# Two-layer encoder on one Trainium2 core: order of gate products, first gather and sums of squares

## What is computed

```python
def encoder_trunk(x, p, W):
    h = x
    for i in range(DEPTH):                       # layer 0: mla_mixer, layer 1: gdn_mixer
        hn = rmsnorm(h, W['norm_mix_g'][i])
        h = h + (mla_mixer if i % 2 == 0 else gdn_mixer)(hn, ...)
        h = h + expert_choice_moe(rmsnorm(h, W['norm_ffn_g'][i]), ...)
        gate = jax.nn.sigmoid(rmsnorm(h, W['norm_ple_g'][i]) @ W['ple_w_gate'][i])
        h = h + (p[i] @ W['ple_w_proj'][i]) * gate
    return rmsnorm(h, W['final_norm_g'])

def expert_choice_moe(h, w_router, w_gate, w_up, w_down):   # 16 experts, 32 tokens of each sequence
    aff = jax.nn.softmax((xt @ w_router), axis=-1)
    gate, idx = lax.top_k(aff.T, cap)
    xe = jnp.take(xt, idx, axis=0)
    hid = silu(xe @ w_gate) * (xe @ w_up)
    ye = (hid @ w_down) * gate[..., None]        # added back at idx

def gdn_mixer(h, w_in, conv_w, A_log, dt_bias, norm_g, w_out):
    # proj = h @ w_in: q, k, v (3072 columns), z (1024), b, a
    # conv of 5 taps and silu on q, k, v; q and k divided by their l2 norm over each head
    # o = chunk_gated_delta forward + backward, rmsnorm(o) * silu(z), @ w_out
```

## Time and profile before

| | us |
|---|---|
| time, median of 3 runs | 1766.92 (1766.44 to 1767.38) |
| the profiled execution's own time | 1766.45 |
| its span, first to last instruction | 1764.7 |
| PE busy | 1636.6 (93% of the span) |
| DVE / ACT / POOL busy | 572.2 / 453.6 / 133.0 |
| mean granted TensorE clock | 0.982 |
| moved by DMA | 450.34 MB, mean 255 GB/s |

### The profile page before, as it was taken

One profiled execution on the slowest core, in us unless ns is written; L12 is line 12 of the kernel. 1 busy time (PEld: TensorE's weight loads), 2 busy tenths in 40 slices (PEclk: granted clock), 3 DMA queues, 4 the chain that ended last, 5 costly groups with the idle time before them and its releaser, 6 DMA issues.

```text
span 1764.7 us, 21301 instructions
## 1 busy us (share of the span) xinstructions
PE 1636.6 (93%) x9045; PEld 847.3 (48%) x9045; DVE 572.2 (32%) x1030; ACT 453.6 (26%) x990; POOL 133.0 (8%) x113
## 2 busy tenths in 40 slices
PE   7999899999889979999999899898999998899788
PEld 4464544443233324578875677854444432333233
DVE  3562311121201213388971356633111212012032
ACT  3232211101011105422125565442111010111053
POOL 2000000000000002052404231000000000000000
PEclk9999999999999999999999999999999999999999
DMA  7008379999999995012120000264799999999931
GB/s 251 1 1 333 120 316 427 427 427 428 427 425 427 428 424 191 1 48 96 50 94 1 1 3 2 97 282 171 286 428 427 427 429 428 424 427 428 426 132 48
DMA packets 50909, 450.34 MB, mean 255 GB/s; under 512 B 4931, under 2 KB 7199, under 8 KB 25599
## 3 DMA queue, kind: packets, MB, share of 16 engines
q1 hardware_dynamic: 50288, 448.67, 61.3%
q0 software_dynamic: 288, 0.22, 0.0%
q10 hardware_dynamic: 239, 0.09, 0.0%
HBM read 446.87 MB, written 2.10 MB: 254 GB/s over the span
## 4 chain that ended last, share of the span: by engine, by line
PE 68%; DMA 15%; DVE 7%; ACT 5%; issue 4%; POOL 1%; SPq 1%; DVEq 0%; ACTq 0%; POOLq 0%
PE banks L1830 28%; PE banks L1241 13%; DMA ring<-in_moe_w_up 7%; PE banks L1369 5%; DMA ring<-in_moe_w_down 5%; PE banks L1463 3%; PE banks L1721 3%; PE banks L1809 3%; PE banks L1858 2%; DVE misc L2171 2%; DMA ring<-in_moe_w_gate 2%; PE banks L1886 2%; PE banks L1324 1%; PE banks L1428 1%; PE banks L1513 1%
## 5 line engine op out<-in xcount | busy, mean ns | idle before, releaser
L1830 PE MATMUL banks<-ring,misc 128*64 128x512 f32 x2048 | 458.2, 598 | 34.0 <-DMA ring<-in_moe_w_up 21.0
L1830 PEld LDWEIGHTS banks<-ring,misc 128*64 128x64 f32 x2048 | 146.6, 138 | 318.3 <-issue 276.6
L1830 PE MATMUL banks<-ring,hid_t 128*64 128x512 f32 x976 | 217.5, 595 | 16.1 <-DMA ring<-in_moe_w_down 13.4
L1241 PE MATMUL banks<-ring,xt 128*128 128x512 f32 (+1 forms) x448 | 189.8, 585 | 1.0 <-ACT xt L830 0.5
L2537 DVE TENSOR_TENSOR work<-work,banks 128x512 f32<-128x512 f32 x32 | 33.6, 1052 | 476.7 <-PE banks L1830 476.7
L1191 ACT ACTIVATE misc<-banks 32x512 f32<-32x512 f32 x64 | 37.6, 587 | 458.3 <-PE banks L1830 457.9
L1830 PEld LDWEIGHTS banks<-ring,hid_t 128*64 128x64 f32 x976 | 68.4, 137 | 155.5 <-issue 138.1
L1241 PEld LDWEIGHTS banks<-ring,xt 128*128 128x128 f32 x448 | 84.8, 190 | 104.0 <-issue 102.9
L2552 DVE COPY misc<-banks 32x512 f32<-32x512 f32 x64 | 44.2, 691 | 226.0 <-PE banks L1830 225.6
L678 POOL TENSOR_TENSOR ring<-ring 128x1024 f32<-128x1024 f32 x24 | 59.6, 2486 | 738.9 <-DMA ring<-in_gdn_w_in 666.4
L2171 DVE SCALAR_TENSOR_TENSOR misc<-ring,conv_w,misc 128x512 f32<-128x512 f32 x96 | 92.2, 960 | 3.4
(11 more groups left out here) (327 smaller groups left out, 1677.0 us busy)
## 6 DMA issues: line engine op xcount, KB each, us to landing
ring<-in_moe_w_gate SPq DMA_DIRECT2D x64, 2048.0 KB, 22.3
ring<-in_moe_w_up SPq DMA_DIRECT2D x64, 2048.0 KB, 24.0
ring<-in_moe_w_down SPq DMA_DIRECT2D x58, 2048.0 KB, 25.0
ring<-in_gdn_w_in SPq DMA_DIRECT2D x8, 2048.0 KB, 8.4
ring<-in_ple_w_gate SPq DMA_DIRECT2D x4, 2048.0 KB, 21.4
ring<-in_moe_w_down SPq DMA_DIRECT2D x6, 1024.0 KB, 23.2
ring<-in_mla_w_out SPq DMA_DIRECT2D x2, 2048.0 KB, 23.4
misc<-in_moe_w_down SPq DMA_DIRECT2D x2, 2048.0 KB, 21.4
```

Source lines behind the costliest of these rows:

```text
L1241: mm = pe.matmul(psum[:, banks.bank(st, i), 0:cols], lhs(k), rhs(k), start=(k == 0), stop=(k == n - 1))
L1830: mm = pe.matmul(psum[64 * f:64 * f + 64, bank, :], tokens(4 * kh + k), w[k][:, k, f * HALF:(f + 1) * HALF], start=(kh == 0 and k == 0), s ...
```

## The change

In three places the order of work is changed. What is computed stays the same.

1. Experts, both layers: part 3 of the first gather runs behind piece 0's products, in front of piece 1's, and the wait for DVE's reading of it stands in front of the seventh of the eight feature blocks. Pieces 9 and 10 trade slots, and SP issues piece 10 (2 MB, into piece 0's slot) ahead of the half of piece 9 (1 MB, into piece 1's).
2. Projection, blocks 1 to 4: the sums of squares run behind P7.
3. Core: the gates stand in portions of three steps and are through before the last two pairs of `build_qk` products of p = 0. On ACT, `end_levels(p)` runs behind the first `spread_u` of the next pass.

PE at the start of the experts of layer 0, before and now. L1809 (now L1808) is the gather, L1830 (now L1831) the products with a piece; 8 matmuls are one piece.

```diff
--- before.py
+++ after.py
@@ -380,7 +380,7 @@
 
             if m == EXTRA:
                 return NSLOT
-            n = m - (m > EXTRA)
+            n = {EXTRA + 1: 9, EXTRA + 2: 8}.get(m, m - (m > EXTRA))
             return place(l, n if n < NARROW else (4, 5, 6, 7, 0, 1)[(n - NARROW) % 6])
 
         def user_before(m):
@@ -426,7 +426,7 @@
                             banks.add(s_bat, 0)
                         if u == 0 and x == P3:
                             banks.add(s_cum, 0)
-                        if 1 <= u <= 4 and x == P2:
+                        if 1 <= u <= 4 and x == P7:
                             banks.add(s_nrm, u - 1)
                         if u == 5 and x == P2:
                             banks.add(s_nt, 0)
@@ -594,7 +594,7 @@
                 sp.wait_ge(*L.s_lg.full(1))
                 src = expert_w["down"][l, 0].rearrange("(a p k) n -> p a k n", a=2, k=4)
                 sp.dma_start(second_down, src[:, 1, 0:2, :]).then_inc(second_in, 16)
-                for m in range(EXTRA + 1, NPIECE):
+                for m in (EXTRA + 2, EXTRA + 1, *range(EXTRA + 3, NPIECE)):
                     if m == NARROW + 7:
 
                         sp.wait_ge(moe_sem["w_used"], last_user(2) + 1 + L.done["w_used"])
@@ -1057,6 +1057,7 @@
                     if live:
                         spread_u(p, 0)
                     if p:
+                        end_levels(prev)
                         keep(apply_banks, "z5", prev, c_z5, 32)
                         spread_inverse(prev)
                     else:
@@ -1110,8 +1111,6 @@
                     if p == 0:
                         gate_in(6)
                         gate_in(7)
-                    if live:
-                        end_levels(p)
 
                 def turned(k):
 
@@ -1397,14 +1396,6 @@
                                                start=True, stop=True)
                         mm.then_inc(s_cum.filled, 1)
                     block_product(u, P2, a12, b21)
-                    if 1 <= u <= 4:
-                        b = u - 1
-                        pe.wait_ge(sq16, 4 * b + 4)
-                        banks.claim(pe, s_nrm, b)
-                        for g in range(4):
-                            mm = pe.matmul(psum[32 * g:32 * g + 32, banks.bank(s_nrm, b), :], pick[:, b, :], sqb[:, g, :],
-                                           start=True, stop=True)
-                        mm.then_inc(s_nrm.filled, 1)
                     if u == 5:
                         s_nrm.wait_read(pe, 3)
                         banks.claim(pe, s_nt, 0)
@@ -1415,6 +1406,14 @@
                         pe.wait_ge(x_comb_pool, 2)
                     pe.wait_ge(w_comb_done, 4 * u + 4)
                     block_product(u, P7, s3, t3)
+                    if 1 <= u <= 4:
+                        b = u - 1
+                        pe.wait_ge(sq16, 4 * b + 4)
+                        banks.claim(pe, s_nrm, b)
+                        for g in range(4):
+                            mm = pe.matmul(psum[32 * g:32 * g + 32, banks.bank(s_nrm, b), :], pick[:, b, :], sqb[:, g, :],
+                                           start=True, stop=True)
+                        mm.then_inc(s_nrm.filled, 1)
                     block_product(u, P4, a22, t4)
 
                 def gate_part(i, k0, k1):
@@ -1641,13 +1640,14 @@
                         dt5(prev)
                     else:
                         gate_part(5, 5, KD)
+                        gate_part(6, 0, 1)
                     if live:
                         level_turn(p, 1)
                         level_z(p, 2)
                     if p:
                         z6(prev)
                     else:
-                        gate_part(6, 0, 2)
+                        gate_part(6, 1, 4)
                         build_kk(1, 0)
                     if p >= 2:
                         for a in range(4):
@@ -1662,7 +1662,7 @@
                     if 1 <= p < QS:
                         du6(prev)
                     elif p == 0:
-                        gate_part(6, 2, 4)
+                        gate_part(6, 4, 7)
                         build_kk(1, 1)
                     if build:
                         build_kk(p + 1, 0)
@@ -1676,7 +1676,8 @@
                         for a in (0, 1):
                             new_values(prev, a)
                     else:
-                        gate_part(6, 4, 6)
+                        gate_part(6, 7, KD)
+                        gate_part(7, 0, 2)
                         build_kk(1, 2)
                     if build:
                         build_kk(p + 1, 1)
@@ -1690,7 +1691,7 @@
                         for a in range(4) if odd else (2, 3):
                             new_values(prev, a)
                     else:
-                        gate_part(6, 6, KD)
+                        gate_part(7, 2, 5)
                         build_kk(1, 3)
                     if build:
                         build_kk(p + 1, 3)
@@ -1703,13 +1704,11 @@
                         for a in range(4):
                             attend(prev, a)
                     else:
-                        gate_part(7, 0, 4)
+                        gate_part(7, 5, KD)
                     if live:
                         build_qk(p, 0)
                         build_qk(p, 1)
                         level_d(p, 4)
-                        if p == 0:
-                            gate_part(7, 4, KD)
                         build_qk(p, 2)
                         build_qk(p, 3)
                 def project_heads(i, half):
@@ -1789,9 +1788,9 @@
                                                start=(t == 0), stop=(t == NT - 1))
                     mm.then_inc(gcol_in, 1)
 
-                def gather(q):
-
-                    for kp in range(4):
+                def gather(q, kps=range(4)):
+
+                    for kp in kps:
                         if q and kp < 2:
                             if q >= 2:
                                 pe.wait_ge(moe_sem["scat_free"], 8 * (q - 1) + L.done["scat_free"])
@@ -1810,7 +1809,7 @@
                                                    start=(t == 0), stop=(t == NT - 1))
                         mm.then_inc(moe_sem["gather_in_psum"], 1)
 
-                def unit_product(kind, n, bank, tokens):
+                def unit_product(kind, n, bank, tokens, ahead={}):
 
                     for kh in range(2):
                         m = piece(kind, n, kh)
@@ -1824,6 +1823,8 @@
                         else:
                             pe.wait_ge(loaded[r], 16 * (L.base[r] + nth_load(l, m)))
                         for k in range(4):
+                            if 4 * kh + k in ahead:
+                                ahead[4 * kh + k]()
                             if k == 2 and m in (EXTRA + 1, NPIECE - 1):
                                 pe.wait_ge(loaded[r], 16 * (L.base[r] + nth_load(l, m)))
                             for f in range(2):
@@ -1887,17 +1888,29 @@
                                            start=(k == 0), stop=(k == 1))
                         mm.then_inc(moe_sem["pp_in_psum"], 1)
 
-                gather(0)
+                def gathered(parts, *engines):
+
+                    for who in engines:
+                        pe.wait_ge(moe_sem["gather_read_" + who], parts + L.done["gather_read_" + who])
+
+                def rest_of_gather():
+
+                    gather(0, (3,))
+                    gathered(2, "act")
+
+                gather(0, (0, 1, 2))
+                gathered(1, "act", "dve")
                 for ex in range(NE + 1):
                     if ex < NE:
                         q, i = ex // GRP, ex % GRP
-                        if i == 0:
+                        if i == 0 and q:
                             for who in ("act", "dve"):
                                 pe.wait_ge(moe_sem["gather_read_" + who], 2 * (q + 1) + L.done["gather_read_" + who])
                         if ex >= 2:
 
                             pe.wait_ge(moe_sem["hid_done"], ex - 1 + L.done["hid_done"])
-                        unit_product("gate", ex, 2 * (ex % 2), lambda k: xg[:, q % 2, k, i, :])
+                        unit_product("gate", ex, 2 * (ex % 2), lambda k: xg[:, q % 2, k, i, :],
+                                     {} if ex else {4: rest_of_gather, 6: lambda: gathered(2, "dve")})
                     if ex:
                         turn_hidden(ex - 1)
                     if ex < NE:
```

## The result

| | before | after |
|---|---|---|
| median, us | 1767.03 (1766.44 to 1767.38, 4 runs) | 1750.79 (1749.03 to 1752.55, 4 runs) |
| the profiled execution's own time | 1766.45 | 1752.55 |
| its span | 1764.7 | 1750.8 |
| PE / DVE busy | 1636.6 / 572.2 | 1636.9 / 575.0 |
| mean granted clock | 0.982 | 0.982 |

What follows compares the result with a forecast made beforehand. Bound: products with expert pieces (28% of the span) and waits for their transfers (14%), elsewhere PE and its waits. Terms 5.0 + 2.0 + 3.9 + 4.6 = 15.5 us, from median 1766.92 to 1751.4; range 1745.5 to 1758.5.

Steps and rivals of the forecast that it cites:

- Stream, 5.0 forecast: Experts' piece transfers: stream starts 2.3 to 2.8 us earlier, taken as 2.5 us a layer, 5.0 for both.
- A gap again, not a larger one than before, or larger by half a us: Experts, first loads: 2 MB then 1 MB are issued before pieces 1 and 2 are used, leaving this transfer gap.
- my lower bound of 2.3: Experts: low end of the 2.3 to 2.8 us a layer by which the stream starts earlier.
- no extra one at 266 us: Experts: piece 10 is used at about 263.7, loads issued last to about 266.7, so its later wait is hidden.
- Projection, 2.0 forecast: Blocks 1 to 4: of 4.6 + 0.6 us about 2.0 remain, since DVE cannot follow; bounds 5.2 and 0.
- the 4.6 us: Projection, block 1: the 3.12 us wait for squares and the low clock behind it go, 4.6 us together.
- Core, p = 0 to 1, 3.9 forecast: Gates end 2.9 us earlier; d of the second level comes at 1010.2 in place of 1014.12, 3.9 us.
- PE has no wait in that pass: Core, p = 0: total of gate products unchanged and PE never waits there.
- the case that DVE's predicated copy is held: Core, p = 0 to 1: copy held until 997.6 by POOL's clearing, `build_qk` waits, turn 1.9 us later, 2.0 remain.
- Core, p = 1 to 3, 4.6 forecast: Two passes: 1.1 us sure at low clock, 3.5 if the clock stays up; one of each, 4.6 us.
- Even at each place: Core, p = 1 to 2 and 2 to 3: even odds that the clock falls behind waits of 0.5 and 1.3 us.
- The first rival: Core: clock falls in both passes and DVE's copy is held, 4.2 in place of 8.5; time 1755.7; chance 0.27.

Runs made afterwards that it cites:

- the first profile: Profile of the whole change against the kernel before, first comparison; ratio 0.9916, median 1750.79 us, the profiled execution 1752.55 us.
- the second: Profile of the whole change measured once more, unaltered, as base of three later kernels; ratio 0.9916 (0.9902 to 0.9931) to the kernel before.

## Why the prediction was right, and where it wasn't

The total held, 15.5 forecast against 14.8 (12.7 to 17.1), and each part gained; but the terms were off on both sides. That the total came within 0.7 us is partly luck: the errors below have both signs, and the terms of the core were reckoned from one profile of before, in which the clock happened to be kind from p = 0 to 1.

**Stream, 5.0 forecast, 4.0 found.** The start was right (2.8, found 2.86). The step that failed is "A gap again, not a larger one than before, or larger by half a us": from the first issue to the last load it takes about 0.9 us longer than before (409.1 to 409.8 us against 408.4 to 408.7). 2.0 us are kept a layer, below my lower bound of 2.3. In the kernel with the stream alone this loss is there by 300 us, so it belongs to the first loads. No second gap came at piece 10, and no extra one at 266 us. The trade of slots, which I had counted into the same sum, is worth 1.3 us a layer, but only together with the moved gather.

**Projection, 2.0 forecast, 2.65 found** (204.10 to 201.44). The mechanism was right and the size of the waits was off: squares late in blocks 2, 3 and 4, POOL's sums over whole convolutions. The waits were 1.2, 0.4 and 0.9 us for my 1.6, 0.5 and 1.3, 2.5 in place of 3.4, and that is the difference; the new waits didn't lower the clock (the interval is 201.41 to 201.44 in four profiles). What I had not seen is how much of the 4.6 us was chance. Waits alone give 3.12 + 0.28 + 0.27 - 2.52 = 1.15 us, which is 202.58 less 201.43; the rest is the low clock behind the old wait, 0 to 2.8 us.

**Core, p = 0 to 1, 3.9 forecast, 3.65 found** (19.44 to 15.40, less 0.39). The 0.39 us are a step I put at nothing ("PE has no wait in that pass"): the first turn of p = 1 comes later (42.58 to 42.97), because PE waits for a bank of `build_qk` that DVE still reads, now that no gate products stand between d and the last pair. I had named this wait, but only for the case that DVE's predicated copy is held. It wasn't: the copy took 0.80 us beside the 3.51 us of clearing, and 0.78 us before, without it:

```profile
991.54 0.78 DVE L2270 COPY_PREDICATED misc<-blocks,misc 128x256 f32<-128x256 uint8 x2 [3.82 <-ACT misc L978]
```
The rule of the Trainium skill (SBUF — State Buffer, "SBUF: two separate sides") holds here, and the rival's half that hung on it didn't come. The 3.65 us are luck in one respect: three profiles with the old gates show 19.4 to 19.5 us at this place, three others 21.1 to 22.0, by the clock behind the same wait of 4.07 us. Against these the change gives 5.3 to 6.3 us. The gates alone leave 17.65 us, with 1.85 us of waiting for ACT's spread, which stands behind end_levels there; with end_levels moved it is 15.40.

**Core, p = 1 to 3, 4.6 forecast, 3.0 in the first profile, 5.9 in the second.** 21.38 to 19.15 and 20.56 to 19.75; then 21.38 to 19.18 and 20.56 to 16.85. With the clock up a pass gives 3.7 us, forecast 3.5. But that is against a pass of before with the clock low; against the two old ones of 18.51 us with the clock up it gives 0.8, what the shorter waits give by themselves. With the clock low I had put 1.1; it was 2.2 at p = 1 to 2, and 0.8 or 2.2 at p = 2 to 3. "Even at each place" was near: of the five profiles with unfilled waits and end_levels moved, the clock stayed up in two at each place. The mean over the table is 20.4 to 18.6 and 20.6 to 18.0, 4.4 us for both. The first rival's condition (clock low in both) is what the first profile shows, though its other half didn't come.

My main mistake of method: I read from one profile of before what a wait costs at the clock, and took it for a property of the wait.

## What to carry to other kernels

Count the wait and the clock behind it apart: here a wait repeats to a tenth of a us, the clock's part is a draw between nothing and its full price, and one profile shows one draw. Where a late operand can't be made earlier, put one more independent product in front of its use before shortening the engine that makes it: here P4 in front of the squares was worth as much as taking POOL's work away. And when a transfer's start is moved forward, look at what the first issue has to bridge: 1 MB in front gave 0.7 us a layer, 2 MB in front 2.0.

## What the runs showed of the hardware

A wait of 3.12 us left the granted clock at 1.00 in one profile, while waits of 0.52 and 1.15 us with small products between them were followed by 0.50 in others; I had expected the longer wait to fall always and the shorter ones by their length. Products that nobody reads, put into the waits of the core, kept the clock up there in the three profiles that have them. DVE's single-input operation with a scalar (L2182), 0.49 us alone, took 1.99 us beside POOL's sums, like the two-input ones behind it, while the predicated copy on SBUF beside POOL's clearing was not slowed (0.80 us, 0.78 without it).
